# Splitting a 512-column product with held weights into two products of 256 columns, each with its own weight load

## What is computed

```python
x = layer_norm(ALPHA * x + mixer(x @ w_in) @ w_out)   # w_in is 2048x5120 (even) or 2048x6144 (odd)
h = jax.nn.relu(x @ w1)                               # w1 is 2048x8192
x = layer_norm(ALPHA * x + (h * h) @ w2)              # w2 is 8192x2048
```

## Time and profile before

| | |
|---|---|
| median of 3 runs | 2257.79 us (2256.98 to 2259.05) |
| span of the profiled execution | 2254.9 us |
| time of the profiled execution outside the span | not recorded; the median of the runs is 2.9 us above the span |
| TensorE products busy | 2171.2 us, 96% of the span, 11058 products |
| TensorE loads busy | 1844.5 us, 82%, 11058 loads |
| VectorE busy | 1476.2 us, 65% |
| ScalarE busy | 1022.0 us, 45% |
| DMA | 181 GB/s on average |

### The profile page before, as it was taken

The page is one execution under the profiler, slowest core; times in us unless marked ns, Lnnn a source line. Parts: engine busy times, 40 slices in busy tenths (PEclk is TensorE's granted clock), DMA queues, the critical chain, the costliest instruction groups (busy, mean ns, idle before and its releaser), DMA issues.

```text
span 2254.9 us, 29169 instructions
## 1 busy us (share of the span) xinstructions
PE 2171.2 (96%) x11058; PEld 1844.5 (82%) x11058; DVE 1476.2 (65%) x1454; ACT 1022.0 (45%) x1224; POOL 128.1 (6%) x48
## 2 busy tenths in 40 slices
PE   7999997999999999999879999997999999999997
PEld 6888886788888888888768888886888888888886
DVE  6766687665666566566876667566666666566657
ACT  4446645344444444444525554553444444444443
POOL 4000023100000000000230000003000000000002
PEclk9999998999999999999989999998999999999999
DMA  8554563555555555555445555454555555555552
GB/s 255 182 169 161 176 227 127 187 188 191 185 193 192 186 186 187 197 176 200 135 168 185 168 174 177 170 169 168 186 186 189 183 195 194 188 184 188 197 192 96
DMA packets 203809, 409.05 MB, mean 181 GB/s; under 512 B 6800, under 2 KB 9088, under 8 KB 202736
## 3 DMA queue, kind: packets, MB, share of 16 engines
q1 hardware_dynamic: 201920, 398.94, 52.8%
q0 software_dynamic: 1840, 9.44, 1.2%
HBM read 406.26 MB, written 2.10 MB: 181 GB/s over the span
## 4 chain that ended last, share of the span: by engine, by line
PE 92%; DVE 5%; issue 1%; SPq 1%; ACT 1%; DMA 1%; DVEq 0%; ACTq 0%
PE ps L690 29%; PE ps L691 15%; PE ps L706 14%; PE ps L708 14%; PE ps L707 14%; DVE w_lo L992 2%; PE ps L694 2%; DVE xT L1022 1%; DMA raw<-in_ev_w_in 1%; PE ps L778 0%; SPq L272 0%; PE ps L819 0%; ACT w_hi L375 0%; PE ps L746 0%; SPq L274 0%
## 5 line engine op out<-in xcount | busy, mean ns | idle before, releaser
L992 DVE TENSOR_TENSOR w_lo<-raw,w_hi 128x1024 fp32r<-128x1024 f32 x752 | 945.2, 1277 | 366.0 <-ACT w_hi L375 365.6
L375 ACT ACTIVATE w_hi<-raw 128x1024 fp32r<-128x1024 f32 x752 | 790.4, 1059 | 848.4 <-PE ps L708 480.7
L690 PE MATMUL ps<-xT,w_hi 128*128 128x512 f32 x2880 | 1044.2, 403 | 60.3 <-DVE xT L1022 45.2
L691 PE MATMUL ps<-xT,w_lo 128*128 128x256 f32 x3072 | 834.8, 282 | 0.0
L690 PEld LDWEIGHTS ps<-xT,w_hi 128*128 128x128 f32 x2880 | 546.8, 190 | 189.5 <-DVE xT L1022 47.1
L691 PEld LDWEIGHTS ps<-xT,w_lo 128*128 128x128 f32 x3072 | 585.5, 191 | 17.1
L706 PE MATMUL ps<-w_hi,yT 128*128 128x512 f32 x1240 | 484.2, 391 | 1.4 <-DVE w_lo L992 1.4
L708 PE MATMUL ps<-w_hi,yT 128*128 128x512 f32 x1240 | 482.7, 389 | 0.0
L707 PE MATMUL ps<-w_lo,yT 128*128 128x512 f32 x1240 | 482.4, 389 | 0.0
L1046 DVE TENSOR_TENSOR res<-ps,res 128x1024 f32<-128x1024 f32 x131 | 160.4, 1224 | 196.7 <-PE ps L708 196.7
L706 PEld LDWEIGHTS ps<-w_hi,yT 128*128 128x128 f32 x1240 | 232.9, 188 | 48.7 <-DVE w_lo L992 1.8
(11 more groups left out here) (183 smaller groups left out, 983.5 us busy)
## 6 DMA issues: line engine op xcount, KB each, us to landing
raw<-in_mlp_w SPq DMA_DIRECT2D x256, 1024.0 KB, 5.0
raw<-in_od_w_in SPq DMA_DIRECT2D x48, 1024.0 KB, 5.1
raw<-in_ev_w_in SPq DMA_DIRECT2D x36, 1024.0 KB, 5.0
raw<-in_ev_w_out SPq DMA_DIRECT2D x16, 1024.0 KB, 5.0
raw<-in_od_w_out SPq DMA_DIRECT2D x16, 1024.0 KB, 5.0
raw<-in_ev_w_in SPq DMA_DIRECT2D x8, 512.0 KB, 12.4
res<-in_x SPq DMA_DIRECT2D x8, 256.0 KB, 9.5
rg<-in_ln_mix_g POOLq DMA_DIRECT2D x2, 1024.0 KB, 4.9
```

The costliest lines, as they stand in the source:

```text
L375: nc.scalar.activation(flat(w_hi[:, k % NSPL]), flat(raw[:, k % NRAW]), ACT.Copy).then_inc(s_hi, 1)
L690: nc.tensor.matmul(ps[:, f], w_hi[:, k % NSPL, i, cols], both, start=first, stop=False)
L691: ins = nc.tensor.matmul(ps[:, f, S:2 * S], w_lo[:, k % NSPL, i, cols], xT[:, rows, 0], start=False, stop=False)
L992: nc.vector.tensor_tensor(flat(w_lo[:, k % NSPL]), flat(raw[:, k % NRAW]), flat(w_hi[:, k % NSPL]).bitcast(F32), ALU.subtract).then_inc(s_ ...
```

## The change

In all pairs but the first and the last of each bank, the 512-column product by `w_hi` is made as two products of 256 columns: one to the left half of the bank from x high, one to the right half from x low. The same stationary operand is loaded for each of the two. The product by `w_lo` stays. The first and the last pair of each bank stay as they were, since they clear or close the whole bank.

```diff
-                        both = xT[:, rows].rearrange("p h s -> p (h s)")
-                        if not last:
-                            nc.tensor.matmul(ps[:, f], w_hi[:, k % NSPL, i, cols], both, start=first, stop=False)
-                        ins = nc.tensor.matmul(ps[:, f, S:2 * S], w_lo[:, k % NSPL, i, cols], xT[:, rows, 0],
-                                               start=False, stop=False)
+                        hi, lo = w_hi[:, k % NSPL, i, cols], w_lo[:, k % NSPL, i, cols]
+                        main, side = ps[:, f, 0:S], ps[:, f, S:2 * S]
+                        if first:
+                            nc.tensor.matmul(ps[:, f], hi, xT[:, rows].rearrange("p h s -> p (h s)"), start=True,
+                                             stop=False)
+                            ins = nc.tensor.matmul(side, lo, xT[:, rows, 0], start=False, stop=False)
+                            continue
                         if last:
-                            ins = nc.tensor.matmul(ps[:, f], w_hi[:, k % NSPL, i, cols], both, start=False, stop=True)
+                            nc.tensor.matmul(side, lo, xT[:, rows, 0], start=False, stop=False)
+                            ins = nc.tensor.matmul(ps[:, f], hi, xT[:, rows].rearrange("p h s -> p (h s)"),
+                                                   start=False, stop=True)
+                            continue
+                        nc.tensor.matmul(main, hi, xT[:, rows, 0], start=False, stop=False)
+                        nc.tensor.matmul(side, hi, xT[:, rows, 1], start=False, stop=False)
+                        ins = nc.tensor.matmul(side, lo, xT[:, rows, 0], start=False, stop=False)
```

## The result

The changed kernel takes **2277.2 us** (median of 4 runs, 2276.47 to 2279.12), the kernel before 2257.76 us (4 runs). The ratio is 1.0086, 95% interval 1.0072 to 1.0100: slower by 0.9%. The forecast was 2276 us, range 2246 to 2331.

A forecast was written before the change was run, and what follows sets the result against it. The prediction took the distances between starts of TensorE's products as the bound. Span 2254.9 + 18.1 for the triples = 2273.0 us, plus 2.9 us of the runs' median above the span, gave 2276 us, range 2246 to 2331.

The forecast's parts named there:

- TensorE's distances are the time: In nearly all of the kernel, time is the sum of distances between starts of TensorE's products; TensorE busy 96%.
- 2688 pairs become triples: In 48 turned blocks, 56 of 64 pairs each gain one product and one load of 128 columns; streamed columns stay 768.
- 120 ns per short product, a triple 360: In turned blocks, 256 columns cost 106.7 ns plus 13.3 per product with its load; a triple is 6.75 ns above the pair.
- the cover of the load: Each short product gives its successor's load 113 to 120 ns to hide in; a bare load takes about 110 ns.
- The rival of the load as the bound: The next load doesn't fit under a short product: 126.6 ns each, a triple 380, +71.5 us, 2329 us; chance 0.12.
- The sum, +18.1 us: 2688 triples in turned blocks, each 6.75 ns above the pair, lengthen the span from 2254.9 to 2273.0 us.
- The 2.9 us outside the span: Added to the forecast span: the runs' median, 2257.8 us, lies 2.9 us above the profiled span, 2254.9.
- The steady pair's extra 6.6 ns: Rival: the steady turned pair's surplus of unknown cause stays in each triple, 366.6 ns, +35.8 us, 2294 us; chance 0.20.
- The rival of the faster side: Alternating long and short costs 2 ns per change in turned blocks; triples have none: -10.8 us, 2247 us; chance 0.14.
- By column: Rival: a short product costs half a long turned one, 117.5 ns, a triple 352.5, -2 us, 2256 us; chance 0.13.
- the small fixed cost: Rival: each split product adds only 2.5 ns, as plain float32 products suggest: 6.7 us, 2264.5 us; chance 0.07.
- The dropped load: Rival: the second load of the same `w_hi` is dropped in each triple: 346.7 ns, -17.6 us, 2240 us; chance 0.01.

The follow-up runs named there:

- mirrored order: Kernel before with the second tile's pair exchanged in every chunk: 512, 256, 256, 512 columns, not 512, 256, 512, 256; 2248.92 us, ratio 0.9960.
- grouped order: Kernel before with each turned chunk's 8 products of 512 columns first and its 8 of 256 behind them; 2253.13 us, ratio 0.9981.

## Why the prediction was right, point by point

- **TensorE's distances are the time.** Right. No new idle time, the natural products at 226.7 ns, the clock mean 0.986 against 0.985, and the other engines only idle longer.
- **2688 pairs become triples.** Right, by the counts.
- **120 ns per short product, a triple 360.** Right to the nanosecond for this size, in the steady blocks, on a ground that holds here by some luck. The ground given, 13.3 ns per product whatever its columns, fits loads of 128 columns with streams of 240 columns and more (within 1.1 ns), and not below: it gives 93.3 ns for 192 columns where 111.7 were measured, and 66.7 for 128 where it was about 115. The prediction called the cover of the load thin and let it be; the runs show how thin: 8 ns. The rival of the load as the bound was therefore near in its ground and wrong for 256 columns: it decides below about 240. One of its figures measures something else: by the prediction's own reading of the earlier trace rows, a plain float32 product takes twice the time of its columns, so the 111 ns of the 18 products of 128 columns are mostly their own 106.7 and needn't tell the length of a load.
- **The sum, +18.1 us.** The span grew by 20.3. The loop's rounds give 6.8 ns per triple, the forecast 6.75; the rest lies outside them. Matched product by product, the two traces show where: the two MLPs, with 1792 triples, took 12.2 us more (12.1 by the forecast's price), the two mixers, with 896, took 8.2 (6.0 by the forecast's price). Of these 2.2 us about 1.0 is known: 160 pairs of the mixers ran in unbroken series at 346.7 ns and became triples of 359.7, so they paid 13.0 ns each and not 6.75. The prediction had read this pace in the earlier trace rows and still counted every pair at 353.25. The other 1.2 us, among pairs beside waits and small products, stay undivided.
- **The 2.9 us outside the span.** They set the median of the runs against the span of another execution. Of one execution the difference is 2277.28 - 2275.2 = 2.1 us. This term made the forecast 0.8 us too long and the sum made it 2.2 us too short; part of the closeness of 2276 to 2277.2 is that the two cancel.
- **The steady pair's extra 6.6 ns.** It didn't stay in the triples, which the forecast assumed without a cause; to that extent it had luck. The mirrored order shows that the order can take it away in the rounds, and the pairs at 346.7 ns show that the order alone doesn't bring it.
- **The rival of the faster side** had a part of the truth. A change of the order alone takes 9 us off, but not by so much per change of size, as the grouped order shows. It lost here because a third product with its load comes in exchange; the mirrored order has the gain without that product.
- **By column** and **the small fixed cost** fall: their triples would have been 352.5 ns and 355.75. The latter came from the plain float32 products of the earlier trace rows, and those are no guide to fp32r ones. The rule of the Trainium skill ("TensorE: Matmul & The Clock Gate", "Back-to-back issue gap"), which that section gives for products without a budget for their loads, doesn't hold for these products with a load each: 226.7 and 120 ns measured where N/2.4 + 2.5 gives 215.8 and 109.2.
- **The dropped load** falls: 13746 loads.

## What to carry to other kernels

Before splitting a product, measure from start to start in groups what a product of the new length costs with its load: here it was 213.3 + 13.3 ns for 512 columns, 106.7 + 13.3 for 256, and a floor of 112 ns at 224 and at 192 columns. Here every further product with its load cost time, and below about 240 columns a shorter stream saved nothing. Where long and short products must alternate, try the order long, short, short, long: it cost nothing here and gained 0.4%.

## What the hardware did that I had not expected

- A product of 128 fp32r columns costs about 115 ns, hardly less than one of 256 (120).
- The surcharge over the columns halved with half the loaded columns in series of 256-column products (13.3 to 6.7 ns; 6.7 with 160 columns too) and grew in series of 512-column ones (13.3 to 16.7 ns).
- With 226.7 ns put down to each long product, one short product between two long ones costs 126.6 ns in the rounds and 120 in the even mixer; two cost (697 - 2 x 226.7) / 2 = 122 ns each, and a steady series 120 each.
- The same alternation of long and short products holds either of two paces for dozens of pairs, 353.3 or 346.7 ns, at the same granted clock of 1.00.
